# Feed-forward first products: input and its remainder as one 512-column product, added up by ScalarE and VectorE

## The reference, cut to what matters

```python
def swiglu_ffn(x, w_gate, w_up, w_down):
    return (jax.nn.silu(x @ w_gate) * (x @ w_up)) @ w_down

x = layer_norm(alpha * x + mix, ln1_g[l], ln1_b[l])
ff = swiglu_ffn(x, w_gate[l], w_up[l], w_down[l])
x = layer_norm(alpha * x + ff, ln2_g[l], ln2_b[l])
```

## Time and profile before

| | us |
|---|---|
| median of 3 runs | 928.84 |
| lowest and highest | 927.58 and 929.49 |
| the profiled execution, its own time | 929.89 |
| its span, first to last instruction | 928.1 |

### The profile page before, as it was taken

One profiled execution on the slowest core, in us unless ns is written; L12 is line 12 of the kernel. 1 busy time (PEld: TensorE's weight loads), 2 busy tenths in 40 slices (PEclk: granted clock), 3 DMA queues, 4 the chain that ended last, 5 costly groups with the idle time before them and its releaser, 6 DMA issues.

```text
span 928.1 us, 13736 instructions
## 1 busy us (share of the span) xinstructions
PE 874.2 (94%) x5592; PEld 722.0 (78%) x5592; DVE 615.1 (66%) x1212; ACT 427.3 (46%) x710; POOL 0.2 (0%) x4
## 2 busy tenths in 40 slices
PE   4899999999999999999999999898988799999996
PEld 1568467766687778777998888788988799999995
DVE  4442857575745669866699989975866745544555
ACT  3352416544632455655444444555643644444441
POOL 0000000000000000000000000000000000000000
PEclk9899999999999999999999999999999799999999
DMA  9675541100363124303665664332446155555541
GB/s 351 260 257 214 203 183 57 46 24 1 113 251 96 44 95 144 95 1 137 185 205 174 200 215 148 123 117 69 140 134 227 59 192 189 174 183 204 175 166 46
DMA packets 39999, 136.71 MB, mean 147 GB/s; under 512 B 4352, under 2 KB 4480, under 8 KB 39680
## 3 DMA queue, kind: packets, MB, share of 16 engines
q1 hardware_dynamic: 38928, 130.48, 41.1%
q10 hardware_dynamic: 1008, 5.36, 1.5%
HBM read 134.77 MB, written 1.05 MB: 146 GB/s over the span
## 4 chain that ended last, share of the span: by engine, by line
PE 78%; DVE 17%; ACT 2%; issue 1%; DMA 1%; SPq 0%; DVEq 0%; ACTq 0%
PE ps L350 9%; PE ps L351 9%; PE ps L355 8%; PE ps L903 6%; PE ps L420 3%; PE ps L422 3%; PE ps L421 3%; PE ps L680 3%; PE ps L448 3%; DVE wlo L1382 3%; DVE AF L1842 2%; PE ps L378 2%; PE ps L703 2%; PE ps L380 2%; PE ps L379 2%; PE ps L367 2%
## 5 line engine op out<-in xcount | busy, mean ns | idle before, releaser
L1382 DVE TENSOR_TENSOR wlo<-raw,whi 128x1024 fp32r<-128x1024 f32 (+2 forms) x204 | 233.4, 1158 | 39.5 <-ACT whi L941 39.3
L941 ACT ACTIVATE whi<-raw 128x1024 fp32r<-128x1024 f32 (+2 forms) x204 | 204.1, 1005 | 105.5 <-DMA raw<-wpack 41.3
L350 PE MATMUL ps<-hh,whi 128*128 128x256 f32 (+1 forms) x736 | 216.1, 294 | 5.9 <-DVE AF L1887 4.8
L351 PE MATMUL ps<-hl,whi 128*128 128x256 f32 (+1 forms) x736 | 212.4, 289 | 0.0
L355 PE MATMUL ps<-hh,wlo 128*128 128x256 f32 (+1 forms) x640 | 184.7, 289 | 0.0
L350 PEld LDWEIGHTS ps<-hh,whi 128*128 128x128 f32 x736 | 140.7, 191 | 11.9 <-issue 7.5
L351 PEld LDWEIGHTS ps<-hl,whi 128*128 128x128 f32 x736 | 140.8, 191 | 3.0 <-issue 0.7
L355 PEld LDWEIGHTS ps<-hh,wlo 128*128 128x128 f32 x640 | 122.4, 191 | 1.4
L420 PE MATMUL ps<-whi,hh 128*128 128x512 f32 (+1 forms) x192 | 70.8, 369 | 0.2 <-ACT acc L1007 0.2
L421 PE MATMUL ps<-wlo,hh 128*128 128x512 f32 (+1 forms) x192 | 70.2, 366 | 0.0
L422 PE MATMUL ps<-whi,hl 128*128 128x512 f32 (+1 forms) x192 | 70.2, 366 | 0.0
(11 more groups left out here) (266 smaller groups left out, 1541.7 us busy)
## 6 DMA issues: line engine op xcount, KB each, us to landing
raw<-wpack SPq DMA_DIRECT2D x178, 512.0 KB, 4.3
AF<-wmod SPq DMA_DIRECT2D x48, 512.0 KB, 6.1
raw<-wpack SPq DMA_DIRECT2D x24, 256.0 KB, 2.9
XT<-xin SPq DMA_DIRECT2D x4, 512.0 KB, 6.0
raw<-wpack SPq DMA_DIRECT2D x4, 432.0 KB, 5.0
uq<-wuq ACTq DMA_DIRECT2D x2, 768.0 KB, 5.6
cst<-cpack ACTq DMA_DIRECT2D x1, 1093.0 KB, 7.8
AF<-wukv ACTq DMA_DIRECT2D x2, 512.0 KB, 7.0
```

Source lines behind the costliest of these rows:

```text
L350: e.matmul(o, wh[:, b], xh(k), start=j == 0, stop=False, skip_group_check=True)
L351: e.matmul(o, wh[:, b], xl(k), start=False, stop=False, skip_group_check=True)
L941: e.activation(W.hi(i), W.raw(i), ACT.Copy).then_inc(*HI.up(j))
L1382: e.tensor_tensor(W.lo(i), W.raw(i), W.hi(i), ALU.subtract).then_inc(*LO.up(j))
```

## The change

For f = 1 to 21 "fg" and "up" are made by a new function, `lin_wide`: per k one matmul with the weights `whi` and 512 columns, 256 of `hh` and 256 of `hl`, into the whole bank of PSUM, and one with `wlo` and the 256 columns of `hh`, added to the left half of the bank. So the left half holds whi·hh + wlo·hh and the right half whi·hl. ScalarE copies each right half to SBUF (`side`), VectorE adds the left half to it; the silu and the product with it now read SBUF. The bank is given back by VectorE's add. `hh` and `hl` become the two halves of one tensor `hx`, so that one access pattern of two stretches, 4096 elements apart, can read both.

```diff
+    def lin_wide(key, wname, cols, xw):
+
+        free = ps.take(key)
+        c, wh, wl = weights(key, (wname, 0, tuple(range(KD)), cols), KD * P)
+        pe.wait_ge(*free)
+        for k in range(KD):
+            b = slice(k * P, (k + 1) * P)
+            pe.wait_ge(xw(k))
+            e.matmul(ps.ap(key, 512).rearrange("p (s n) -> p s n", s=2), wh[:, b], K.hx[:, :, k, 0:256], start=k == 0, stop=False, skip_group_check=True)
+            i = e.matmul(ps.ap(key, 256), wl[:, b], hh[:, k, 0:256], start=False, stop=k == KD - 1, skip_group_check=True)
+        i.then_inc(*M.up(key))
+        W.given[c] = M.now()
@@ tensor_program, f > 0
-            lin(("fg", f), "w_ffn_gate_2", 0, cc, range(KD), x2h, x2l, 256, xt3)
-            lin(("up", f), "w_ffn_up_2", 0, cc, range(KD), x2h, x2l, 256, xt3)
+            lin_wide(("fg", f), "w_ffn_gate_2", cc, xt3)
+            lin_wide(("up", f), "w_ffn_up_2", cc, xt3)
@@ scalar_program
         highs(("fg", m))
+        side = K.AF[:, 8192 + 2 * z:8704 + 2 * z]
         ac.wait_ge(M["fg", m], V["fu", m - 2] if m >= 2 else None)
-        e.activation(K.AF[:, z:z + 256], ps.ap(("fg", m), 256), ACT.Silu).then_inc(*A.up(("fg", m)))
-        ps.give(("fg", m), A.now())
+        if m == 0:
+            e.activation(K.AF[:, z:z + 256], ps.ap(("fg", m), 256), ACT.Silu).then_inc(*A.up(("fg", m)))
+            ps.give(("fg", m), A.now())
+        else:
+            e.activation(side[:, 0:256], ps.ap(("fg", m), 256, 256), ACT.Copy).then_inc(*A.up(("fgs", m)))
+            ac.wait_ge(V["fga", m])
+            e.activation(K.AF[:, z:z + 256], side[:, 0:256], ACT.Silu).then_inc(*A.up(("fg", m)))
         highs(("up", m))
+        if m:
+            ac.wait_ge(M["up", m])
+            e.activation(side[:, 256:512], ps.ap(("up", m), 256, 256), ACT.Copy).then_inc(*A.up(("ups", m)))
@@ vector_program
-        dv.wait_ge(M["up", m], A["fg", m], V["f", m - 2] if m >= 2 else None)
-        e.tensor_tensor(h, K.AF[:, z:z + 256], ps.ap(("up", m), 256), ALU.mult).then_inc(*V.up(("fu", m)))
-        ps.give(("up", m), V.now())
+        side = K.AF[:, 8192 + 2 * z:8704 + 2 * z]
+        if m == 0:
+            ...
+        else:
+            dv.wait_ge(A["fgs", m])
+            e.tensor_tensor(side[:, 0:256], side[:, 0:256], ps.ap(("fg", m), 256), ALU.add).then_inc(*V.up(("fga", m)))
+            ps.give(("fg", m), V.now())
+            dv.wait_ge(A["ups", m])
+            e.tensor_tensor(side[:, 256:512], side[:, 256:512], ps.ap(("up", m), 256), ALU.add).then_inc(*V.up(("upa", m)))
+            ps.give(("up", m), V.now())
+            dv.wait_ge(V.now(), A["fg", m], V["f", m - 2] if m >= 2 else None)
+            e.tensor_tensor(h, K.AF[:, z:z + 256], side[:, 256:512], ALU.mult).then_inc(*V.up(("fu", m)))
@@ build
-        K.hh = sb("hh", [P, KD, TT], F32R)
-        K.hl = sb("hl", [P, KD, TT], F32R)
+        K.hx = sb("hx", [P, 2, KD, TT], F32R)
+        K.hh, K.hl = K.hx[:, 0, :, :], K.hx[:, 1, :, :]
```

More of the change, by code:

```diff
@@ L2010, in vector_program @@
         h = K.AF[:, 512 + z:768 + z]
-        dv.wait_ge(M["up", m], A["fg", m], V["f", m - 2] if m >= 2 else None)
-        e.tensor_tensor(h, K.AF[:, z:z + 256], ps.ap(("up", m), 256), ALU.mult).then_inc(*V.up(("fu", m)))
-        ps.give(("up", m), V.now())
+        side = K.AF[:, 8192 + 2 * z:8704 + 2 * z]
+        if m == 0:
+            dv.wait_ge(M["up", m], A["fg", m])
+            e.tensor_tensor(h, K.AF[:, z:z + 256], ps.ap(("up", m), 256), ALU.mult).then_inc(*V.up(("fu", m)))
+            ps.give(("up", m), V.now())
[5 more added lines that the diff above has]
+            e.tensor_tensor(side[:, 256:512], side[:, 256:512], ps.ap(("up", m), 256), ALU.add).then_inc(*V.up(("upa", m)))
+            ps.give(("up", m), V.now())
+            dv.wait_ge(V.now(), A["fg", m], V["f", m - 2] if m >= 2 else None)
+            e.tensor_tensor(h, K.AF[:, z:z + 256], side[:, 256:512], ALU.mult).then_inc(*V.up(("fu", m)))
         dv.wait_ge(A["f", m])
```

## The result

Measured with 20 runs each, the changed kernel takes 927.01 us (925.82 to 928.83) and the kernel before 929.63 (927.58 to 933.59). The ratio is 0.9974, with an interval from 0.9966 to 0.9982: faster by 0.26%, or 2.4 us of 928.84 (1.7 to 3.2). The way was right, the size was not: I had 4.5 us.

A forecast was written before the change was run, and what follows sets the result against it. TensorE's stream was taken to bound the feed-forward; 336 dropped fixed parts of 0.0135 us save 4.5 us, all else costs nothing: 928.84 - 4.5 = 924.3 us. The 8-in-10 range was 920.9 to 927.6 us.

The forecast's parts named there:

- What bounds the kernel: Feed-forward: TensorE alone, 8.50 us a round, so a nanosecond off its stream is a nanosecond of the kernel.
- Step 1: Rounds 1 to 21: three narrow matmuls become one wide and one narrow, 0.360 to 0.3465 us, 336 times, 4.5 us saved.
- rival (a): Narrow-to-wide edge: the surcharge stays and no discount returns; pair 0.355 us, gain 1.7 us, 927.1 us; chance 0.12.
- The second stretch: Wide matmul's moving operand read in two stretches of 256 columns: costed at nothing, from fp32 rows of 592 and 593 ns.
- (b): Wide matmuls: the fixed part goes with each 256-column stretch, not the instruction; pair stays 0.360 us, time 928.8 us; chance 0.08.
- (c): Wide matmuls: the jump to the second stretch restarts the stream; pair 0.4165 us, 19 us more, 947.8 us; chance 0.08.
- The estimate by the Trainium skill: The 336 dropped matmuls: about 2.5 ns each beyond their columns, 0.8 us in all, no difference.
- Step 2: Copies and adds in 21 rounds: ScalarE 16 us and VectorE 18 us more, silu 0.9 us later, beside TensorE, costing nothing.
- Step 3: End of the last round: the chain to block 21 gets 0.9 us longer, still 0.5 us early for TensorE; costs nothing.
- The numbers: Whole kernel: forecast 924.3 us with chance 0.72; faster 0.78, same 0.14, slower 0.08; range 920.9 to 927.6 us.

The follow-up runs named there:

- e1: Changed kernel with the input's rounded half and its rest in one stretch of 512 elements, alternation kept: 8.386 us a round, ratio 0.9977 to the kernel before.
- e2: Changed kernel with the eight wide matmuls of a product first and its eight narrow ones behind: 8.306 us a round, ratio 0.9959 to the kernel before.
- e7: Changed kernel with "fg" wide ones first and "up" narrow ones first, two changes of width a round: 8.287 us a round, ratio 0.9952 to the kernel before.
- e3: Changed kernel with three narrow matmuls per k block, the added ScalarE and VectorE work kept: 8.499 us a round, ratio 0.9999 to the kernel before.
- e5: The changed kernel itself, run once more: 8.387 us a round, ratio 0.9968 to the kernel before.

## Why the prediction was wrong in size

**What bounds the kernel**: right. The chain of waits and the stretches of after show TensorE alone, and a saving in its stream came out of the measured time in full: 2.4 us by rounds, 2.4 by runs.

**Step 1** failed, in one term: the price of the pair. The prediction read both edges out of the earlier trace rows, 0.235 for a wide one behind a narrow one and 0.11 for a narrow one behind a wide one, and said that they "nearly cancel". It took the first matmul behind each edge for the whole edge. They don't cancel even once, and the earlier trace rows had it: from 866.19 to 868.94 twelve wide ones take 2.75 us where settled ones take 2.72, and from there to the next `down`, at 866.19 + 8.50, 48 narrow ones take 5.75 where settled ones take 5.76. That is 0.03 lost and 0.01 given back. In the strict alternation the wide ones keep a mean surcharge of 0.0097 and the narrow ones a mean discount of 0.0030. The pair is 0.3533, the saving 0.0067 instead of 0.0135 us a pair, and 336 x 0.0067 = 2.3 us instead of 4.5. The safer reading was in the text as the bound and as rival (a), 0.355 and 1.7 us: the pair measured lies next to it. That rival had a chance of 0.12. Its reason (every wide matmul in the alternation stands behind a narrow one) is what e1, e2 and e7 show to be the cause; that no discount comes back is not so, since a third of the surcharge does.

**The second stretch**, cost at nothing by the fp32 rows, was right, also at the full column rate: e1 against the changed kernel, 8.386 and 8.386 us a round. Rivals (b) and (c) fall with it. The fixed part of 0.0135 us does go with the instruction and not with the stretch: all wide, with two stretches in each, takes 0.2267 a step. The estimate by the Trainium skill (TensorE: Matmul & The Clock Gate, section Back-to-back issue gap), 0.8 us for 336 matmuls at the price of an isolated one, is a third of what the changed kernel gained and a fifth of what its better order did; the measurement decides.

**Step 2** was right in its consequence and nearly in size: 16.2 us more for ScalarE where I had 16, and 16.0 for VectorE where I had 18. VectorE's 42 adds alone take 17.7 us (21 of 0.420 and 21 of 0.421), so the rest of the difference between the two pages lies in its other work. Timeline of ScalarE, then of VectorE, in one round of after:

```profile
770.76 0.38 ACT L1370 ACTIVATE AF<-ps 128x256 f32<-128x256 f32 x1 [1.69 <-PE ps L394]
771.63 0.42 ACT L1372 ACTIVATE AF<-AF 128x256 f32<-128x256 f32 x1 [0.49 <-DVE AF L2040]
771.95 1.04 ACT L954 ACTIVATE whi<-raw 128x1024 fp32r<-128x1024 f32 x1
```

```profile
765.62 0.42 DVE L2043 TENSOR_TENSOR AF<-AF,ps 128x256 f32<-128x256 f32 x1 [2.41 <-ACT AF L1376]
766.08 0.42 DVE L2046 TENSOR_TENSOR AF<-AF 128x256 f32<-128x256 f32 x1
767.33 3.49 DVE L1404 TENSOR_TENSOR wlo<-raw,whi 128x1024 fp32r<-128x1024 f32 x3
771.17 0.42 DVE L2040 TENSOR_TENSOR AF<-AF,ps 128x256 f32<-128x256 f32 x1 [0.35 <-ACT AF L1370]
```

Silu starts 0.87 us behind the copy, where I had 0.9; the one price that was off is that of silu out of SBUF, 0.42 where I took 0.38 as out of PSUM. VectorE now makes its three `wlo` in one piece. None of it is waited for by TensorE, and e3 shows the whole of it to cost nothing.

**Step 3** was right. The end of the last round, VectorE and TensorE:

```profile
907.57 0.63 PE L916 MATMUL ps<-whi,hx 128*128 128x512 f32 x2
...
909.90 1.22 DVE L1404 TENSOR_TENSOR wlo<-raw,whi 128x1024 fp32r<-128x1024 f32 x1
```

The last `wlo` ends at 911.12, 3.55 us behind the first `down` product of the end ("about 3.5"). TensorE wants it at 907.57 + 18 x 0.2267 = 911.65 and has it 0.5 us early.

**The numbers.** The measured median, 927.01 us, lies in the range given, because the range took in (a) and not because the forecast's pair was right; the movement of 2.4 us is little over half of the forecast's. The absolute forecast was also set against a median of three runs, 928.84, which the 20 runs later put at 929.63.

## What to carry to other kernels

Where TensorE's stream is the bound, price a matmul by the distance of starts in a settled row of its own kind, and then ask what stands ahead of it in the new order: a price read in a row of equals does not hold in an alternation. At an edge, add up all steps until the row has settled, not the first alone, and compare whole groups; and if the new groups are shorter than that, no such sum can be trusted and the order has to be run. Here 512-column fp32r matmuls belong in long rows of their own, or in twos; by the traces the same instructions in another order gave nearly twice the gain. And when a saving is some microseconds of 930, read the stage in the trace: the executions differ by more than that before they come to it.

## What the runs showed that I had not expected

A full-width fp32r matmul (512 columns) behind one of 256, 320 or 384 columns costs 0.23 to 0.24 us to the next start instead of 0.2267, and the shorter one doesn't give all of it back in a strict alternation: 0.0067 us more a pair at 512/256, and 0.007 at 512/320 and 512/384. At 384/256 it gives all of it back. Behind a row of narrow ones the surcharge lasts for five wide ones. Of the orders with groups, two pairs lose little (8.294 us a round), four more (8.353), eight less again (8.306), and one change each way least (8.287). Why the full width differs, and why the loss doesn't fall with the number of changes, stays open: the profile has no row for what TensorE does between two starts, and no run was made between 384 and 512 columns.

The entry into the stage varies from execution to execution, by more than the change gains. The transposes behind round 0, up to which all variants do the same work, stand between 735.36 us (e5) and 740.48 (groups of four), and at 738.27 and 735.36 in two executions of the same kernel.
